# Four unused SBUF tensors in a one-core two-block transformer kernel: other start offsets for weights and SwiGLU buffers

## The reference

```python
x = x + 0.5 * _swiglu(_rmsnorm(x, ffn1_norm[l]), gate1[l], up1[l], down1[l])   # D_FF = 2816
h = _rmsnorm(x, mix_norm[l]); p = h @ w_in[l]                                    # 2244 columns
out = [sliding-window heads, block-selected heads, top-k-selected heads](p)
x = x + concat(out) @ w_out[l]
x = x + 0.5 * _swiglu(_rmsnorm(x, ffn2_norm[l]), gate2[l], up2[l], down2[l])
# _swiglu(x) = (silu(x @ w_gate) * (x @ w_up)) @ w_down
```

## Time and profile before

| | us |
|---|---|
| median of 3 runs | 4569.96 (4564.29 to 4571.83) |
| profiled execution, span from its first to its last instruction | 4562.2 |
| PE busy in the span | 4098.9 |
| PE weight loads busy | 3310.5 |
| DVE busy | 2465.4 |
| ACT busy | 1586.1 |
| POOL busy | 1214.7 |

### The profile page before, as it was taken

The page is one execution under the profiler, slowest core; times in us unless marked ns, Lnnn a source line. Parts: engine busy times, 40 slices in busy tenths (PEclk is TensorE's granted clock), DMA queues, the critical chain, the costliest instruction groups (busy, mean ns, idle before and its releaser), DMA issues. The chain is left out here.

```text
span 4562.2 us, 54694 instructions
## 1 busy us (share of the span) xinstructions
PE 4098.9 (90%) x19818; PEld 3310.5 (73%) x19818; DVE 2465.4 (54%) x3644; ACT 1586.1 (35%) x2660; POOL 1214.7 (27%) x764
## 2 busy tenths in 40 slices
PE   5999989899699989889997999879999778888999
PEld 3877777678577768757775887758888557666887
DVE  4775375775577646567643245344554444353555
ACT  2222344222222232622225555332222374643332
POOL 5883004992389500199600000000000000000000
PEclk9999799899899988989998999989999888898999
DMA  6443112333344311034321111011121110101332
GB/s 220 132 131 99 41 43 74 101 129 101 119 151 133 107 56 60 24 98 137 111 74 54 52 52 33 15 64 61 60 64 46 52 34 9 33 6 56 97 96 78
DMA packets 99856, 354.09 MB, mean 78 GB/s; under 512 B 11139, under 2 KB 14723, under 8 KB 98776
## 3 DMA queue, kind: packets, MB, share of 16 engines
q1 hardware_dynamic: 76632, 274.64, 18.5%
q0 software_dynamic: 18304, 70.33, 4.9%
q10 hardware_dynamic: 4736, 6.62, 0.4%
HBM read 345.73 MB, written 11.06 MB: 78 GB/s over the span
## 5 line engine op out<-in xcount | busy, mean ns | idle before, releaser
L173 DVE TENSOR_TENSOR w_lo<-w_raw,w_hi 128x1024 fp32r<-128x1024 f32 x500 | 888.8, 1778 | 1194.5 <-ACT w_hi L166 1193.8
L166 ACT ACTIVATE w_hi<-w_raw 128x1024 fp32r<-128x1024 f32 x500 | 530.5, 1061 | 2106.0 <-PE ps L197 1946.4
L195 PE MATMUL ps<-h_hi,w_hi 128*128 128x512 f32 (+1 forms) x2824 | 1118.0, 396 | 111.4 <-DVE h_lo L254 84.3
L196 PE MATMUL ps<-h_lo,w_hi 128*128 128x512 f32 (+1 forms) x2824 | 1104.2, 391 | 0.0
L197 PE MATMUL ps<-h_hi,w_lo 128*128 128x512 f32 (+1 forms) x2824 | 1101.9, 390 | 0.0
L195 PEld LDWEIGHTS ps<-h_hi,w_hi 128*128 128x128 f32 x2824 | 542.5, 192 | 258.9 <-DVE h_lo L254 69.3
L1197 POOL TENSOR_TENSOR shared<-shared 128x1024 f32<-128x1024 f32 (+5 forms) x480 | 631.1, 1315 | 41.5 <-POOL shared L1197 15.2
L197 PEld LDWEIGHTS ps<-h_hi,w_lo 128*128 128x128 f32 x2824 | 543.4, 192 | 118.0
L196 PEld LDWEIGHTS ps<-h_lo,w_hi 128*128 128x128 f32 x2824 | 544.0, 193 | 113.1 <-issue 1.4
L195 PE MATMUL ps<-a_hi,w_hi 128*128 128x512 f32 x1472 | 550.6, 374 | 22.2 <-DVE x L450 18.8
L197 PE MATMUL ps<-a_hi,w_lo 128*128 128x512 f32 x1472 | 549.8, 374 | 0.0
(11 more groups left out here) (238 smaller groups left out, 5010.5 us busy)
## 6 DMA issues: line engine op xcount, KB each, us to landing
w_raw<-in_w_first SPq DMA_DIRECT2D x316, 512.0 KB, 3.6
w_raw<-in_w_mlp SPq DMA_DIRECT2D x128, 512.0 KB, 3.5
shared<-in_w_ada POOLq DMA_DIRECT2D x96, 512.0 KB, 3.9
w_raw<-in_w_odd SPq DMA_DIRECT2D x30, 512.0 KB, 3.5
w_raw<-in_w_even SPq DMA_DIRECT2D x26, 512.0 KB, 3.5
near_stage<-near_bias POOLq DMA_DIRECT2D x32, 256.0 KB, 2.9
bias_rows<-bias_line SPq DMA_DIRECT2D x1, 5120.0 KB
shared<-silu_cond POOLq DMA_DIRECT2D x4, 1024.0 KB, 5.5
```

Of the source, the lines that this page charges most:

```text
L166: act.activation(self.hi[:, n % H, :], self.raw[:, n % R, :], ACT.Copy).then_inc(self.hi_done, 1)
L173: dve.tensor_tensor(self.lo[:, n % self.n_hl, :], self.raw[:, n % self.n_raw, :], self.hi[:, n % self.n_hl, :].bitcast(F32), ALU.subtract) ...
L195: pe.matmul(out, lhs[0], rhs[0], start=start, stop=False)
L196: pe.matmul(out, lhs[0], rhs[1], start=False, stop=False)
```

## The change

Four tensors are allocated that nothing reads or writes: 248 floats (992 bytes) per partition ahead of the weight rings of the first block, 432 floats (1728 bytes) ahead of `mid`, `val`, `a_hi` and `a_lo` of the first block, 496 floats (1984 bytes) ahead of the rings of the even layer, 248 floats ahead of the rings of the odd layer. 

```diff
@@ first_layers
+            sb(ctx, "same_offset", [128, 248])
             st = Stream(ctx, S, io["w_first"], 3, 3, LAYER1_TILES)
@@ first_layers
+            sb(ctx, "same_offset", [128, 432])
             mlp_a = Mlp(ctx, S, st, 0, [stream], True, lambda s, o: 0.5)
@@ even_layer
+                sb(ctx, "same_offset", [128, 496])
                 st = Stream(ctx, S, io["w_even"], 3, 2)
```

## The result

The changed kernel took 4517.1 us, median of 4 executions (4511.51 to 4530.28), the kernel before 4567.12 (4562.61 to 4571.83). The ratio is 0.99, 95% interval 0.9879 to 0.9921. Its profiled execution was its longest: 4530.28 us, span 4528.7. The same kernel in two later comparisons stood at 4506.81 and 4504.92 us, ratios 0.9873 (0.9856 to 0.989) and 0.9865 (0.9844 to 0.9885). So it is faster by some 50 to 60 us, where 38.6 were forecast.

A forecast was written before the change was run, and what follows sets the result against it. PE's own pace was taken to bound the MLPs and projections. Pace terms summed to 40.6 us, less 2 us for DVE waits: 38.6 us off 4569.96 gives 4531 us, own range 4522 to 4541, 8-in-10 range 4519 to 4551.

The forecast's parts named there:

- The pace of `h` and `a` in the MLPs: Four SwiGLU MLPs for `h`, first block for `a`: equal offsets save 6.6 and 2.3 ns per full-clock matmul, 27.2 + 4.8 us.
- The projections: First block's projections: 1104 `h` matmuls, 91% at full clock, each 6.6 ns shorter, 6.6 us gained.
- The even layer: Pad three: `h` gains 3.2 us, settling after 256-column runs loses 0.6, slower 256-column matmuls lose 3.5.
- The odd layer: Pad four: matmuls on `h` and `cq` gain 2.9 us, if PE is on the path there.
- the prediction's first rival: DVE takes the gain beside GpSimd: half of the first block's gain is given back, 4549 us; chance 0.14.
- 128-column matmuls: Short matmuls with weights moving, 224 x 3: between 4.1 us lost and 4.4 us gained, taken as zero.
- The waits for DVE: At L450 PE waits for DVE's addition into x; 2 us of PE's gain is given back there.
- the sentence of "TensorE: Matmul & The Clock Gate": Loading next weights takes no SBUF read bandwidth from the running matmul; by it the pads would gain zero.
- That the offset is not the cause: Rival: four ring slots or absent GpSimd make the MLP layers fast, the pads do nothing, 4570 us; chance 0.07.
- That the pace doesn't settle: Rival, first block's MLPs: equal offsets stay in the slow starting state, making `h` and `a` slower, 4591 us; chance 0.05.

The follow-up runs named there:

- light kernels: GpSimd's conditioning products cut to 32 columns (result wrong): with the offsets of the kernel before, 4475.15 us; with all four pads, 4433.38 us.
- the mix: Against the changed kernel: distance 192 in the even layer and in the MLP layer on x and context; 4503.13 us, ratio 0.9866 to the kernel before.
- the sweep: Three kernels giving every stage other weight-to-operand distances than the kernel before: 4540.72, 4568.23 and 4578.64 us, beside 4563.4 of the kernel before.

## Why the prediction was right, and where its size was off

**The pace of `h` and `a` in the MLPs, 27.2 + 4.8 us.** Right. The mean fast step went from 231.9 to 226.8 ns, times some 6180 of them 31.5 us, and 33.0 us in the light kernels' stages.

**The projections, 6.6 us.** Right: 7.1 us less in the two mixers.

**The even layer, 3.2 - 0.6 - 3.5 = -0.9 us.** Right in its parts: `h` settles to 226.7, `c` pays; the layer stays as it was to 0.4 us, and the ratio with pads three and four alone is 1.0003. One count was off: 24 x 3 of the 192 x 3 matmuls with `c` moving are the odd layer's, 0.3 us at 4 ns each.

**The odd layer, 2.9 us.** The condition "if PE is on the path there" failed. The layer in two stretches, first in the light kernel with the offsets of before:

```profile
3488.00:3555.00 67.00, 49.97 (x200) 35.44 (x200) 33.94 (x43) 33.41 (x52) 0.00 (x0) 0.86 0.15 47
3555.00:4095.00 540.00, 448.25 (x2324) 347.17 (x2324) 229.70 (x517) 286.40 (x437) 0.00 (x0) 0.88 0.08 26
```

and in the light kernel with the pads:

```profile
3448.00:3514.00 66.00, 48.79 (x200) 35.19 (x200) 33.77 (x42) 33.14 (x51) 0.00 (x0) 0.87 0.16 48
3514.00:4056.00 542.00, 446.26 (x2324) 346.26 (x2324) 229.46 (x517) 285.99 (x436) 0.00 (x0) 0.88 0.08 26
```

PE is busy 498.2 and 495.1 us, 3.1 less, as forecast, but the layer takes 1 us more. In the waits (time, number, longest) one of the layer's grew. The kernel before:

```profile
PE ps L584 <- DVE q L908: 13.9, 2, 7.7
```

and the changed kernel:

```profile
PE ps L584 <- DVE q L908: 16.0, 2, 8.4
```

Here PE waits for the rotated `q`, which DVE writes at its own time, and waits 2.1 us longer. That is not the whole cause, and not in every trace. With all four pads again, with pads three and four alone and with the mix, the same wait is 13.0 us, less than before, and the layer takes 610 to 611 us all the same: there PE is busy longer, at a lower granted clock. The layer in the kernel before:

```profile
3579.00:4186.00 607.00, 496.31 (x2525) 380.19 (x2525) 263.35 (x558) 319.45 (x486) 0.00 (x0) 0.89 0.09 28
```

and with all four pads again:

```profile
3536.00:4146.00 610.00, 502.12 (x2525) 386.91 (x2525) 262.92 (x558) 318.82 (x486) 0.00 (x0) 0.86 0.09 28
```

Over all traces the layer takes 606.4 to 610.6 us in four kernels at the old distance and 607.9 to 611.8 in six at 0. So the gain is given back, partly to a wait for DVE, as in the prediction's first rival, and partly to time at half clock; what decides between them isn't traced. The shortest odd layers on record are those of the sweep at 64 and 192, 602.3 and 603.4 us, in one execution each: in this layer 0 was not shown to be the best distance.

**128-column matmuls, 0 us.** Right: 316 and 317 ns of mean.

**The waits for DVE, -2 us.** This is the term that failed. The pace terms sum to 40.6 us and the light kernels measure 41.8. With GpSimd at its work the pads are worth 50 to 60 us, so that what lies beside GpSimd gave some 8 to 20 us where 2 were to be lost; that is why the first median is 14 us below the forecast and 2 us under the low end of the range. I took the waits as the 18.8 us of the row for L450 and let them grow. In the changed kernel's first trace they did, to 22.4 us, but over six traces with `h` at 0 they are 11.8 to 22.4, mean 15.9, against 18.8 and 19.8 in two with `h` as before. But GpSimd's products cost the kernel before 92.6 us (4567.73 - 4475.15) and the changed one 71.5 (4504.92 - 4433.38). The wait itself is the small part. Beside it stand the slow splits and the time at half clock (the 1.2 GHz level), 13 to 31 us in each SwiGLU MLP of the kernel before and 3 to 5 in the light one; what share of the 92.6 us each has was not separated.

The Trainium skill's page "SBUF — State Buffer", section "Who interferes with whom", allows DVE and GpSimd to block each other through one shared port pair and excludes any other contention. The first half agrees: DVE's split takes 1778 ns of mean over the kernel before (2192 in its SwiGLU MLPs, beside the products) and 1231 over the light one. The second half and the sentence of "TensorE: Matmul & The Clock Gate" that the prediction weighed don't fit what is measured here: a step of TensorE depends on the distance between its own two operands, by up to 7.5 ns in 227. That its two reads get in each other's way is what this suggests; no row shows a read itself.

**What stays open** is why the faster pace makes this load cheaper. The traces at hand don't show it: the profiled spans of six kernels with `h` at 0 in the first block average 4519.7 us (4501.6 to 4532.3), 41.7 below the 4561.4 of two with `h` as before (4562.2 and 4560.6), which is the pace alone, though spans that scatter like this leave room. The 24 executions of those six without a profile average 4507.1 us (standard deviation 7), against 4564.5 (36 executions of the other two, 8). So the surplus of some 15 us shows in executions of which no trace is kept. The profiled execution is the longest of its kernel in four of the six; whether profiling itself takes part of the gain was not tested. In the traces, the cost of GpSimd per MLP scatters: 15.1, 23.9, 26.8 and 26.5 us in the kernel before, 21.7, 29.1, 15.1 and 29.8 in the changed one (each less the same MLP of its light kernel). That PE's waits then fall at other moments is a guess; no run tells it from others.

**The rivals.** That the offset is not the cause fell with the sweep. That the pace doesn't settle fell with the first block's timeline. That DVE takes half of the first block's gain fell there; only in the odd layer was the gain given back, and there not to DVE alone.

## What to carry to other kernels

Where PE streams pairs of weight load and 512-column matmul without a gap, place both operands at the same offset modulo 256 bytes (seen here for fp32r). By the period found, an unused tensor of under 256 bytes ahead of one of them would do it; here equal offsets took 6.7 of 233.4 ns off a step of `h`. Where short runs of 512 columns alternate with 256, try 192 as well: it was the better distance for that layer. Read it off the distance between starts of a settled run, compared between stages, not off the mean of a group, which mixes clocks. Count the gain only where PE is never idle; where a wait for DVE or ACT follows, the time goes into the wait, and where GpSimd loads the core as well, a gain or loss of PE may come out some ten microseconds larger or smaller than its count.

## What the runs showed of the hardware that had not been expected

- The period is 256 bytes, not the 2048 of a row or the 512 that rows of before suggested. Of the multiples of 32 tried, 0 is the best distance for unmixed runs of 512 columns (226.7 ns), 192 the next (229.0), all others are at 232 to 234.
- For 256 columns the order turns over: 120 ns at 0, 116 to 118 at 192, 114 to 117 at 64.
- The weight load's own duration is the same, 188 ns, at fast and slow distances, and its start lies some 3 ns from a matmul's start. So the load as recorded is not what is stretched.
- GpSimd's conditioning products, on the least busy engine (27%), cost the kernel before 92.6 us, more than this change brings.
